# The first modulation and norm of a two-block network: loads in 4 KB rows, another order of the sums, the mean square as a column

## What is computed

```python
c_act = jax.nn.silu(c)
mod = (c_act @ w_mod[l] + b_mod[l])[:, None, :]
sh1, sc1, g1, sh2, sc2, g2 = jnp.split(mod, N_MOD, axis=-1)
h = rms_norm(x) * (1.0 + sc1) + sh1      # x * rsqrt(mean(x*x) + eps)
proj = h @ w_in[l]
u, v, z, xbc, dt_raw, gate_a, gate_b = jnp.split(proj, offs, axis=-1)
```

## Time and profile before

| | us |
|---|---|
| median of 3 runs | 927.41 |
| lowest and highest | 926.66 and 929.55 |
| span of the profiled execution | 925.2 |
| PE, DVE, ACT, POOL busy in it | 915.6, 706.2, 565.7, 100.7 |

### The profile page before, as it was taken

One profiled execution on the slowest core, in us unless ns is written; L12 is line 12 of the kernel. 1 busy time (PEld: TensorE's weight loads), 2 busy tenths in 40 slices (PEclk: granted clock), 3 DMA queues, 4 the chain that ended last, 5 costly groups with the idle time before them and its releaser, 6 DMA issues.

```text
span 925.2 us, 17436 instructions
## 1 busy us (share of the span) xinstructions
PE 915.6 (99%) x6700; PEld 845.9 (91%) x6700; DVE 706.2 (76%) x952; ACT 565.7 (61%) x827; POOL 100.7 (11%) x88
## 2 busy tenths in 40 slices
PE   9999999999999999999999999999999999999997
PEld 6799999999999989989888888999879999999886
DVE  5957888889988968568777556689886798877663
ACT  4376655687877765456555345566665776666453
POOL 0000300024423300010000001403100200000001
PEclk9999999999999999999999999999999999999999
DMA  9954455577767756545655655535423365655661
GB/s 355 361 177 156 163 193 182 180 234 258 228 232 250 245 175 209 183 147 174 201 186 188 194 186 183 162 134 183 136 92 117 116 200 186 202 182 183 195 210 48
DMA packets 85564, 175.53 MB, mean 190 GB/s; under 512 B 5424, under 2 KB 46912, under 8 KB 85504
## 3 DMA queue, kind: packets, MB, share of 16 engines
q1 hardware_dynamic: 84384, 172.12, 56.2%
q10 hardware_dynamic: 752, 1.27, 0.4%
q0 software_dynamic: 368, 1.31, 0.4%
HBM read 173.63 MB, written 1.05 MB: 189 GB/s over the span
## 4 chain that ended last, share of the span: by engine, by line
PE 96%; DVE 2%; ACT 1%; POOL 0%; issue 0%; DVEq 0%; POOLq 0%
PE proj_ps L1665 18%; PE proj_ps L1682 17%; PE proj_ps L1666 17%; PE proj_ps L1667 17%; PE proj_ps L1685 9%; PE proj_ps L1754 1%; PE aux L1795 1%; PE proj_ps L1755 1%; PE proj_ps L1756 1%; PE aux L1786 1%; PE aux L2084 1%; PE aux L2111 1%; PE aux L1948 1%; DVE mod_acc L992 1%; PE aux L1810 1%; PE aux L1942 1%
## 5 line engine op out<-in xcount | busy, mean ns | idle before, releaser
L980 DVE TENSOR_TENSOR w_lo<-raw,w_hi 128x1024 fp32r<-128x1024 f32 x276 | 343.2, 1256 | 125.7 <-ACT w_hi L491 125.2
L491 ACT CAST w_hi<-raw 128x1024 fp32r<-128x1024 f32 x276 | 286.1, 1047 | 171.0 <-PE proj_ps L1667 70.4
L1665 PE MATMUL proj_ps<-act_pair,w_hi 128*128 128x256 f32 x1016 | 289.9, 285 | 0.0
L1667 PE MATMUL proj_ps<-act_pair,w_lo 128*128 128x256 f32 x1016 | 287.3, 283 | 0.0
L1666 PE MATMUL proj_ps<-act_pair,w_hi 128*128 128x256 f32 x1016 | 287.3, 283 | 0.0
L1665 PEld LDWEIGHTS proj_ps<-act_pair,w_hi 128*128 128x128 f32 x1016 | 194.7, 192 | 3.7 <-issue 1.5
L1666 PEld LDWEIGHTS proj_ps<-act_pair,w_hi 128*128 128x128 f32 x1016 | 194.8, 192 | 0.6
L1667 PEld LDWEIGHTS proj_ps<-act_pair,w_lo 128*128 128x128 f32 x1016 | 194.7, 192 | 0.0
L1682 PE MATMUL proj_ps<-ff_pair,w_hi 128*128 128x512 f32 x256 | 69.9, 394 | 0.0
L1682 PE MATMUL proj_ps<-act_pair,w_hi 128*128 128x512 f32 x248 | 67.7, 394 | 0.0
L439 POOL TENSOR_TENSOR tmp_b<-tmp_b 128x512 f32<-128x512 f32 x4 | 5.2, 1294 | 458.4 <-ACT tmp_b L514 458.4
(11 more groups left out here) (355 smaller groups left out, 1639.0 us busy)
## 6 DMA issues: line engine op xcount, KB each, us to landing
raw<-in_panels SPq DMA_DIRECT2D x308, 512.0 KB, 3.6
mod_first<-in_panels SPq DMA_DIRECT2D x16, 512.0 KB, 10.3
xres<-in_x_t SPq DMA_DIRECT2D x2, 512.0 KB, 5.5
wst<-in_ws_t POOLq DMA_DIRECT2D x1, 512.0 KB, 3.8
bs_sb<-in_bs_rows POOLq DMA_DIRECT2D x1, 512.0 KB, 4.6
level_sb<-in_levels ACTq DMA_DIRECT2D x1, 512.0 KB, 5.4
out_t<-tmp_a SPq DMA_DIRECT2D x1, 512.0 KB, 2.6
out_t<-tmp_a SPq DMA_DIRECT2D x1, 384.0 KB, 3.0
```

The source lines that it names most:

```text
L491: nc.scalar.copy(w_hi[:, s, :], raw[:, s, :]).then_inc(hi_done, 1)
L980: tt(out=w_lo[:, s, :], in0=raw[:, s, :], in1=w_hi[:, s, :].bitcast(F32), op=ALU.subtract).then_inc(taken, 1)
L1665: mm(dst, hi, xh, start=first and k == 0 and nt % 2 == 0, stop=False, skip_group_check=True)
L1667: ins = mm(dst, lo, xh, start=False, stop=last and k == ks - 1, skip_group_check=True)
```

## The change

- **Loads.** `mod_first` is laid out so that each row of a load, 4 KB in memory, is also 4 KB in a piece in SBUF; before, it went to two places of 2 KB. The last two loads of half 1 have a semaphore each (`mod_left`, `mod_in[3]`).
- **Sums.** In half 1 DVE takes tiles 0, 1, 2, 4 and 6, tile 6 in two halves of 512 columns, and PE 3, 5 and 7. In half 2 PE takes tile 7 and DVE 0 to 6. Closing and bias go by pairs of K tiles (four times instead of two), in two PSUM banks.
- **Mean square** as a column of two elements; root and reciprocal on two elements; PE spreads the result to a row by two products with the identity (L1802 of the new file), and ACT copies it to `diag`. ACT loads the identity itself, behind `cols`; POOL loads the rest of `square` with the tables, after the eighth raw panel instead of the fourth.
- **Panels.** `early_panel` replaces `token_panel` for the eight panels of v: four products of high parts, which wait only for the high parts, then the four with low activations and the four with low weights (in the second panel the other way round). ACT makes the first two high parts before the second panel's cast.
- **Order.** DVE makes the norm in pairs, with the low parts of the panels between; in half 2 the sums move behind the low parts. PE closes half 2 after the sixth panel instead of before it. Most of the warming products go.

```diff
-PE_MOD = (0, 1, KT - 1)
-DVE_MOD = range(2, KT - 1)
+PE_MOD = (3, 5, KT - 1)
+DVE_MOD = (0, 1, 2, 4, KT - 2)
+FIRST_NTS, LATER_NTS = (0, 1, 4, 5), (2, 3, 6, 7)
...
-        mod_first = at("mod_first", 72, [N_MOD_FIRST, 1024])
+        mod_first = at("mod_first", 72, [N_MOD_FIRST // 2, 2, 2, 512])
...
-                        dst = mod_first[:, half * KT + 2 * r:half * KT + 2 * r + 2, 512 * a:512 * a + 512]
-                        sp.dma_start(dst, panels[(2 * a + half) * SLOTS + r].rearrange("p (k n) -> p k n", k=2)
-                                     ).then_inc(mod_in[half * (KT // 2) + r], 16)
+                        landing = mod_left if (half, r, a) == (0, 3, 0) else mod_in[half * (KT // 2) + r]
+                        sp.dma_start(mod_first[:, half * (KT // 2) + r, a].rearrange("p k n -> p (k n)"),
+                                     panels[(2 * a + half) * SLOTS + r]).then_inc(landing, 16)
...
-            pool.wait_ge(landed[3], 16)
-            pool.dma_start(square[:], square_d).then_inc(S["early_in"], 16)
             pool.wait_ge(landed[3], 2 * 16)
...
+            for dst, src in ((square[:, 0:2], square_d[:, 0:2]), (square[:, 3:4], square_d[:, 3:4]), (wst[:], ws_t), (bs_sb[:], bs_rows)):
+                pool.dma_start(dst, src).then_inc(S["sgu_in"], 16)
...
+            for dst, src in ((cols[:], cols_d), (ident, square_d[:, 2])):
+                act.dma_start(dst, src).then_inc(S["cols_in"], 16)
...
-            act.wait_ge(S["ms_mm"], 1)
-            nc.scalar.activation(flat(diag[:]), aux[:, 2, 0:T], ACT.Sqrt, bias=eps[:]).then_inc(S["rt_done"], 1)
+            root(0)
+            act.wait_ge(S["rs_mm"], 1)
+            nc.scalar.copy(flat(diag[:]), aux[:, 2, 0:T]).then_inc(S["c_ready"], 1)
             nc.scalar.activation(exp_a[:], col("a_log", 0, HEADS), ACT.Exp).then_inc(S["c_ready"], 1)
             split_hi(0, 0)
+            norm_hi(0, lambda k: modc[:, k:k + 1], lambda k: None, range(2))
             split_hi(0, 1)
-            norm_hi(0, lambda k: modc[:, k:k + 1], lambda k: None, range(4))
+            norm_hi(0, lambda k: modc[:, k:k + 1], lambda k: None, range(2, 4))
...
+            def mod_first_panel(half, k):
+                dve.wait_ge(mod_in[half * (KT // 2) + k // 2], 32)
+                count = len(DVE_MOD) + 2 + k if half else DVE_MOD.index(k) + 1
+                mod_panel(mod_first[:, half * (KT // 2) + k // 2, :, k % 2], k, S["mod_acc_ok"], count, acc=mod_halves)
+            def mod_last_panel(a):
+                dve.wait_ge(*((mod_left, 16), (mod_in[KT // 2 - 1], 16))[a])
+                mod_panel(mod_first[:, KT // 2 - 1, a, 0], KT - 2, S["mod_acc_ok"], len(DVE_MOD) + a, acc=mod_halves[:, a])
...
-            dve.wait_ge(S["rt_done"], 1)
-            step(nc.vector.reciprocal(flat(diag[:]), flat(diag[:])))
-            for n in DVE_MOD:
-                mod_first_panel(n)
-            dve.wait_ge(x_in[0], 16)
+            mod_first_panel(0, 0)
+            inverse(0, stat[:, 1]).then_inc(S["rs_done"], 1)
+            for k in DVE_MOD[1:-1]:
+                mod_first_panel(0, k)
+            for a in range(2):
+                mod_last_panel(a)
+            def first_scaled(pair):
+                mod_first_evac(pair)
+                dve.wait_ge(x_in[pair // 2], 16)
+                dve.wait_ge(S["c_ready"], 2)
+                for k in (2 * pair, 2 * pair + 1):
+                    stt(out=tmp_a[:, k], in0=xres[:, k], scalar=modc[:, 8 + k:9 + k], in1=flat(diag[:]), op0=ALU.mult,
+                        op1=ALU.mult).then_inc(S["nrm_t"], 1)
+            def first_low(pair):
+                for k in (2 * pair, 2 * pair + 1):
+                    dve.wait_ge(S["nrm_hi"], k + 1)
+                    dve.wait_ge(S["nrm_t"], k + 1)
+                    stt(out=act_lo[:, k], in0=tmp_a[:, k], scalar=modc[:, k:k + 1], in1=act_hi[:, k].bitcast(F32),
+                        op0=ALU.add, op1=ALU.subtract).then_inc(S["nrm_lo"], 1)
+            first_scaled(0)
+            first_low(0)
             split_lo(0, 0)
-            def first_norm(half):
-                norm_apply(0, lambda k: modc[:, 8 + k:9 + k], lambda k: modc[:, k:k + 1], lambda k: split_lo(0, 1) if k == 1 else None,
-                           range(4 * half, 4 * half + 4), flat(diag[:]))
-            mod_first_evac(0)
-            first_norm(0)
-            mod_first_panel(KT)
+            first_scaled(1)
...
+            def mod_tile(half, k, nts, first=False):
+                for nt in nts:
+                    mm(first_cols(half)[nt], mod_first[:, half * (KT // 2) + k // 2, nt // 4, k % 2, nt % 4 * P:nt % 4 * P + P],
+                       silu_c[:, k:k + 1], start=first and nt in (0, 2), stop=False, skip_group_check=True)
...
-                ins = mm(aux[:, 2, 0:T], avg_d[:], tmp_b[:, k], start=k == 0, stop=k == 6)
+                for t in range(TT):
+                    ins = mm(aux[:, 2, t:t + 1], tmp_b[:, k, t * P:t * P + P], avg_d[:, 0:1], start=k + t == 0, stop=k == 6,
+                             skip_group_check=True)
...
+            keep_warm(1)
+            pe.wait_ge(S["cols_in"], 32)
+            row_of(0, bank=2)
+            keep_warm(2)
+            for k in PE_MOD[:-1]:
                 pe.wait_ge(mod_in[k // 2], 32)
-                for nt, dst in enumerate(first_cols(0)):
-                    mm(dst, mod_first[:, k, nt * P:nt * P + P], silu_c[:, k:k + 1], start=k == 0 and nt == 0, stop=False, skip_group_check=True)
-                    if nt % 4 == 3 and k < 2:
-                        keep_warm(1)
-                if k == 1:
-                    keep_warm(1)
+                mod_tile(0, k, range(8), k == PE_MOD[0])
+                keep_warm(1)
+            pe.wait_ge(mod_left, 16)
+            mod_tile(0, KT - 1, (0, 1))
             pe.wait_ge(S["mod_acc_ok"], len(DVE_MOD))
-            mod_sum(first_cols(0), first=False)
-            keep_warm(2)
+            mod_sum(first_cols(0), False, (0, 1))
+            pe.wait_ge(mod_in[KT // 2 - 1], 16)
+            mod_tile(0, KT - 1, (4, 5))
+            pe.wait_ge(S["mod_acc_ok"], len(DVE_MOD) + 1)
+            mod_sum(first_cols(0), False, (4, 5), (5,))
+            mod_tile(0, KT - 1, LATER_NTS)
+            mod_sum(first_cols(0), False, LATER_NTS)
...
+            def early_panel(n, k0, par, first, w_low_last):
+                s = n % SLOTS
+                part = lambda a, k, t: a[:, k0 + k, t * P:t * P + P]
+                of_w = lambda w, k: w[:, s, k * 512:k * 512 + 512]
+                bank = lambda t: proj_ps[:, par, t * 512:t * 512 + 512]
+                pe.wait_ge(hi_done, n + 1)
+                for k in range(2):
+                    pe.wait_ge(S["nrm_hi"], k0 + k + 1)
+                    for t in range(TT):
+                        mm(bank(t), part(act_hi, k, t), of_w(w_hi, k), start=first and k == 0, stop=False, skip_group_check=True)
+                for w_low in ((False, True) if w_low_last else (True, False)):
+                    if w_low:
+                        pe.wait_ge(taken, n + 1)
+                    else:
+                        pe.wait_ge(S["nrm_lo"], k0 + 2)
+                    for k in range(2):
+                        for t in range(TT):
+                            ins = mm(bank(t), part(act_hi if w_low else act_lo, k, t), of_w(w_lo if w_low else w_hi, k),
+                                     start=False, stop=False, skip_group_check=True)
+                ins.then_inc(used, 1)
...
-                    if (half, n) == (0, N_HALF - 1):
-                        keep_warm(1, 0)
-                        pe.wait_ge(S["mod_acc_ok"], KT + len(DVE_MOD))
-                        mod_sum(first_cols(1), nts=range(4))
-                        keep_warm(1, 0)
-                        mod_sum(first_cols(1), nts=range(4, 8))
-                    if n < 2:
-                        pe.wait_ge(S["nrm_lo"], k0 + 2)
                     if n < 4:
-                        token_panel(at_n // SLOTS, at_n % SLOTS, n // 2, k0, k0 == 0, k0 == 6)
+                        early_panel(at_n, k0, n // 2, k0 == 0, n != 1)
                     else:
                         panel(at_n // SLOTS, at_n % SLOTS, 0, act_hi, act_lo, k0, k0 == 0, k0 == 6, acc=u0_ps)
+                    if (half, n) == (0, N_HALF - 1):
+                        pe.wait_ge(mod_in[KT - 1], 32)
+                        mod_tile(1, KT - 1, FIRST_NTS, True)
+                        pe.wait_ge(S["mod_acc_ok"], len(DVE_MOD) + KT)
+                        mod_sum(first_cols(1), False, FIRST_NTS, (5,))
+                        mod_tile(1, KT - 1, LATER_NTS, True)
+                        mod_sum(first_cols(1), False, LATER_NTS)
                     if (half, n) == (1, 0):
                         pe.wait_ge(S["narrow_ok"], 1)
+                        pe.wait_ge(S["mod_done"], MOD_EARLY)
```

96 lines of the change are left out of this document (45 added, 51 removed).

## The result

The changed kernel takes 934.24 us (median of 4 runs, 933.35 to 935.14) against 927.95 (the same kernel as before, now with a fourth run): ratio 1.0067, 95% interval 1.0051 to 1.0084. Run again later, beside other experiments, it took 933.83 us, ratio 1.0072 (1.0052 to 1.0091). The forecast was 927.3 with a range up to 928.9. The profiled execution spans 931.4 us, 6.2 more than before's 925.2.

A forecast was written before the change was run, and what follows sets the result against it. PE's own work was taken as the bound, moved only by the eighth panel's start. The head's 4.0 us lead shrank to 2.0 at the fifth panel, 1.0 at the seventh, 0.1 at the eighth: 927.3 us, range 925.6 to 928.9.

The forecast's parts named there:

- The mark and what bounds the kernel: PE only works from the eighth panel's start (49.86 us) on, so the whole time moves by what that start moves.
- The head: Start up to the first panel: modulation sums start earlier, first panel product at 20.4 instead of 24.44, 4.0 us ahead.
- Two closing products, 4 of the 16 records that take 1.93 us: PE's closing of the first modulation part, before the first panel: 0.5 us after DVE's last sum, done at 18.8.
- The dropped warming products ran beside this, in time in which PE had nothing else: PE before the first panel: the dropped warming products filled otherwise empty time; no gain counted for dropping them.
- The first four panels: Same 48 products, 11.9 us before; about 1 us of new waits, end near 32.3, so the lead halves.
- The fifth panel: Its load decides: landing at 32.2, start at 34.6, 2.0 us ahead, after PE stands for about 2 us.
- The rows of 4 KB: Longer load rows: 416 GB/s against 408, 2%, or 0.2 us on the eight loads.
- Half 2: Second modulation: DVE's sums end at 42.2, its norm chain at 48.85, using up the rest of the lead.
- PE beside that: PE from fifth to eighth panel: seventh near 45.0, 1.0 us ahead; wait of 1.0 to 1.2; eighth at 49.8.
- Where POOL's instruction falls: Begins some 0.2 us after the last norm; the step width's low part goes free, the next split pays.
- The third, halved clock on dense work: Rival: half-clock stretches on panels, 1.7 us each; one (or POOL's meeting) up to 928.9, 0.16; two 930.7, 0.06.
- POOL's meeting: POOL's instruction lengthens the step width's low part by 0 to 0.9 us; 0.16 together with one half-clock stretch.

The follow-up runs named there:

- a2: The changed kernel with one warming product after the squares of tile 1 and one after those of tile 3: 932.84 us, ratio 1.0053.
- c1: The changed kernel with the edits of a2 and a4 and two warming products after the first quarter of half 1's tile 7: 928.37 us, ratio 1.0000.
- a1: The changed kernel with tile 7 of half 2 summed by DVE instead of PE: 931.73 us, ratio 1.0038.
- b1: The kernel before with tile 7 of half 2 moved from DVE to PE: 929.94 us, ratio 1.0023.
- c5: c2 with PE's one-column products of half 2's tile 7 put ahead of the sixth panel instead of behind it: 927.33 us, ratio 1.0001.
- a3: The changed kernel without the two warming products behind the row products and the two between half 1's tiles: 933.23 us, ratio 1.0049.
- b2: The kernel before with half 1's tiles 3, 5 and 7 on PE and 0, 1, 2, 4 and 6 on DVE: 938.41 us, ratio 1.0109.
- c2: c1 with the step width's low part made before the eighth panel's on DVE, and that panel taking low weights last: 929.08 us, ratio 1.0013.
- u3: The changed kernel with half 1's tiles shared as before, plus the edits of a1 and a2: 930.03 us, ratio 1.0029.
- c4: c2 with tile 7 of half 2 summed by DVE instead of PE: 929.72 us, ratio 1.0018.
- c3: c2 with one warming product added in the middle of each of the two closings: 930.45 us, ratio 1.0017.
- a5: The changed kernel with the first pair's 16 closing records of half 2 moved into the middle of the sixth panel: 933.46 us, ratio 1.0068.
- a4: The changed kernel with tile 5 of half 1 summed by DVE instead of PE, without the warming product behind it: 929.33 us, ratio 1.0017.
- u1: The changed kernel with half 1's tiles shared as before, PE summing 0, 1 and 7 and DVE 2 to 6: 934.66 us, ratio 1.0079.

## Why the prediction was wrong, step by step

**The mark and what bounds the kernel**: right in kind, and then not followed into the first 50 us, where the sum let DVE and the loads decide. The time moved by what the eighth panel moved, 5.7 of 6.2 us.

**The head, forecast 20.4, measured 27.57**: this step failed, in three terms. (1) "Two closing products, 4 of the 16 records that take 1.93 us", 0.5 us: I took the first pair's records and let the first panel follow. On PE, in order, 32 one-column records stand between the last warming products and that panel; at 0.112 us each, as in the earlier trace rows and here, that is 3.6 us at the full clock. (2) I had PE free when the last tile lands. It was 4 us behind in the changed kernel (21.74 against 17.62) and 1.8 in a2 at the full clock, since nothing in the text added up PE's list from 9 us on. Where the clock holds, the first panel comes at 22.93 (a2), 2.5 us later than forecast by the amount alone. (3) The other 4.6 us, the changed kernel's profile against a2's, go with the clock. "The dropped warming products ran beside this, in time in which PE had nothing else" looked at the time they took and not at the clock they held; the squares as columns took six wide products (twelve records, 3.14 us from 7.42 in the kernel before) out of the same place. That "most of the warming products go" is too strong besides: of nine behind the squares five stay, all in the head.

**The first four panels**: 13.47 us instead of the 11.9 used, because 5.3 us of them ran at 0.50. (The forecast's own terms, 11.9 less half of 0.8 and 1 more for waits, give 12.5 and an end at 32.9, not 32.3; it changed nothing, as the load came later.) **The fifth panel**: landing right (32.42 in a2; 32.44 in the changed kernel), its consequence right wherever PE was early enough to meet it (a wait of 0.68 in c1, forecast 2), and void in a2 (35.55 without a wait) and in the changed kernel, which came to it at 41.04. **The rows of 4 KB** brought nothing to the eight loads: tile 7 lands at 17.62 by its semaphore against 17.48.

**Half 2**: the chain on DVE was right to 0.2 us (a2), and so was PE's one-column work: "about 3.5 us as before" is 3.56 in a2 and 3.79 in the changed kernel, 0.6 of it at the half clock. What the text did not see is that the two warming products that go would have left PE some 1.7 us ahead, and that tile 7's 16 records, 1.8 us, take just this: giving it back to DVE brought 2.5 us (a1), putting it alone on PE cost 2.4 (b1). The norm's chain behind the closing started 5.2 us later than forecast only because PE came late. **PE beside that**: "the seventh panel starts near 45.0" is 45.16 in a2, in part by luck, since there PE came later to the fifth panel and waited for nothing, where the forecast had it early and waiting; in the changed kernel it is 50.59.

**Where POOL's instruction falls**: without effect on PE here, and otherwise than I said. In the changed kernel it began at 53.91, 0.2 us after the step width's low part (53.69), and took

```profile
53.91 4.55 POOL L396 TENSOR_SCALAR_AFFINE_SELECT wst<-wst 128x1024 f32<-128x1024 f32 x1 [11.54 <-DVE act_pair L1131]
```

instead of 1.11 us, while DVE's three low parts beside it took 3.49 us together, 1.16 each, undisturbed. So it is POOL that stood still this time; I had said that the next low part would pay. It did in the kernel before and in c5 (POOL 1.14 us from 47.83, DVE's four low parts 5.51 together), although POOL began 0.2 us behind the step width's part in all three. The rule of the Trainium skill (SBUF — State Buffer, Who interferes with whom), that one of the two blocks wholly, agrees with all three; that it is the one which issues second tells too little where DVE's instructions follow each other, and no run here shows what decides.

**Rivals.** The third, halved clock on dense work, is what happened, and I gave it 0.22 (POOL's meeting among it) with 1.7 us a stretch. Its price was too low in two ways: a stretch was taken as 3.41 us long, as the one in the trace, and they are up to 10.2 (in a3 23.9); and one-column work was left out of it, though on a PE with no slack it doubles too. I also let a stretch before 20.4 vanish "in the wait for the fifth panel", which held only if PE was ahead. The rule of the Trainium skill (TensorE: Matmul & The Clock Gate, HAM oscillation — how this bites in real kernels), that the clock falls in gaps of idleness, is not borne out by the changed kernel: at 22.7 and at 50.0 it fell with no idle time on PE since 9.21, after mostly one-column products. The changed kernel's first fall (9.01, in a wait of 0.67 us) and b2's (15.04, 2.5 us behind one of 1.93) could be read either way. The Trainium skill (TensorE: Matmul & The Clock Gate, What's actually happening) also says that one kernel starts with more or fewer slow products from run to run; the traces agree, since the six warming records at the very start, the same in all kernels, took from 4.30 us (c2) to 5.49 us (the kernel before). That is 1.2 us, less than the 6.4 us by which a2's executions differ.

**What stays open.** One-column products stand ahead of nearly every fall, with or without warming products among them. What keeps the clock up is not settled: with warming products among the squares the profiles of a2, c1 and c5 have it at 1.00 up to the first panel, those of u3 and c4 have a fall at 14.9 and 18.5 all the same, and of a2's ten executions only three have a mean clock of 0.994 or more; one in the middle of a closing did not keep it in c3's profile, and closings of 1.8 us kept it in c5's and not in c4's or u3's. a5, which cut the stretch with nothing else changed, gave too little to tell. So the clock's share of the loss is read from profiles and mean clocks, and the amount's from edits (a1, a4, b1). Nor is it shown why PE's stop before L1688 at 350 us is longer than before, or why u3, in which PE has the tiles of the kernel before in both halves, keeps 2.7 us of the loss where c1 keeps none.

## What to carry to other kernels

Before a wait is removed, add up the list of the engine that is to profit, from its last idle time to the mark, at both of its clocks: if it exceeds what the wait covered, nothing is gained, and moving work onto that engine costs its full length. A stage that is filled with warming products is not spare: the work that replaces them takes its full length, and the clock of the dense work behind may change with it. And where single executions of one program differ by 6 us, compare their mean clocks first, up to the end of the program.

## What the runs showed of the hardware

- A one-column fp32 record (128x1) takes 0.112 us at the full clock and 0.213 at the half one, spaced back to back; so products with next to no columns double as well.
- The granted clock fell with PE busy for the whole stretch before (22.7 and 50.0 us), and then stayed at 0.50 for 10.2 and 3.4 us (in u1, from 10.2 us on, for 27.3), also under dense products: in the changed kernel 5.3 us of panels passed before it rose at 32.9.
- Ten executions of one program spanned 927.66 to 934.10 us, with mean clocks of 0.997 to 0.987 (a2).
- In the first microseconds the clock column shows less than the records do: the first warming records of the kernel before are spaced 0.86 us apart, twice the 0.43 of the full clock, in windows (2 to 6 us) in which it reads 1.00.
- POOL's select beside DVE's low parts took 4.55 us with these undisturbed, or 1.11 with the next of them at 2.11 instead of 1.2: one of the two stands still, and from the same start it was now the one, now the other.
